# High and low weight parts interleaved element by element in one buffer, in a one-core decoder step

## What is computed

```
proj = rmsnorm(x) @ w_in          # 2048 -> 7168: short convolution and retention, 8 heads
out  = concat(y_conv, y_ret) @ w_out
x    = x + out
q    = rmsnorm(x) @ w_q           # product-key router: 8 heads, top 16 of 16384 experts each
hid  = gelu(h @ u_tab.T)          # here for all 16384 experts, gates are 0 for those not picked
x    = x + (gate * hid) @ v_tab   # then a last rmsnorm
```

## Time and profile before

| what | value |
|---|---|
| time, median of 3 runs | 2122.25 us (2121.98 to 2123.11) |
| span of the profiled execution | 2120.7 us |
| TensorE matmul busy | 2099.2 us, 99% |
| TensorE weight load busy | 2087.6 us, 98% |
| VectorE busy | 1441.5 us, 68% |
| ScalarE busy | 963.0 us, 45% |
| GpSimd busy | 68.4 us, 3% |

### The profile page before, as it was taken

The page is one execution under the profiler, slowest core; times in us unless marked ns, Lnnn a source line. Parts: engine busy times, 40 slices in busy tenths (PEclk is TensorE's granted clock), DMA queues, the critical chain, the costliest instruction groups (busy, mean ns, idle before and its releaser), DMA issues.

```text
span 2120.7 us, 46483 instructions
## 1 busy us (share of the span) xinstructions
PE 2099.2 (99%) x18585; PEld 2087.6 (98%) x18585; DVE 1441.5 (68%) x2700; ACT 963.0 (45%) x1343; POOL 68.4 (3%) x94
## 2 busy tenths in 40 slices
PE   8999999999999999999999999999999999999997
PEld 8999999999999999999999999999999999999997
DVE  8888876568888677755656656565645556666665
ACT  6666533444534344443434344443434344444444
POOL 1111000000000000000000000000000000000000
PEclk9999999999999999999999999999999999999999
DMA  8666555654455556675556565565656566656653
GB/s 296 222 217 216 189 180 182 199 176 152 159 188 179 179 189 213 207 245 184 195 198 212 187 213 196 195 204 194 212 188 205 174 216 203 215 202 201 205 180 123
DMA packets 115175, 418.39 MB, mean 197 GB/s; under 512 B 13600, under 2 KB 14112, under 8 KB 114752
## 3 DMA queue, kind: packets, MB, share of 16 engines
q1 hardware_dynamic: 100800, 365.29, 52.2%
q0 software_dynamic: 9888, 34.47, 5.0%
q10 hardware_dynamic: 4320, 16.22, 2.0%
HBM read 391.55 MB, written 24.29 MB: 196 GB/s over the span
## 4 chain that ended last, share of the span: by engine, by line
PE 98%; DVE 1%; ACT 0%; DMA 0%; issue 0%; DVEq 0%; SPq 0%; ACTq 0%
PE bank L929 32%; PE bank L930 31%; PE bank L931 31%; PE bank L1102 2%; PE bank L1057 1%; DVE wlo L1181 0%; PE bank L1002 0%; DMA acc<-xT 0%; DVE acc L1871 0%; PE bank L1013 0%; PE bank L1009 0%; PE bank L977 0%; PE bank L987 0%; PE bank L961 0%; DVE outer L1273 0%
## 5 line engine op out<-in xcount | busy, mean ns | idle before, releaser
L1181 DVE TENSOR_TENSOR wlo<-raw,whi 128x1024 fp32r<-128x1024 f32 x688 | 830.5, 1223 | 500.4 <-ACT whi L634 496.5
L634 ACT CAST whi<-raw 128x1024 fp32r<-128x1024 f32 x688 | 710.2, 1048 | 630.8 <-PE bank L931 624.7
L929 PE MATMUL bank<-xhi,whi 128*128 128x264 f32 x3200 | 911.5, 285 | 0.0
L930 PE MATMUL bank<-xlo,whi 128*128 128x264 f32 x3200 | 906.7, 283 | 0.0
L931 PE MATMUL bank<-xhi,wlo 128*128 128x264 f32 x3200 | 906.5, 283 | 0.0
L930 PEld LDWEIGHTS bank<-xlo,whi 128*128 128x128 f32 x3200 | 603.1, 188 | 0.0
L929 PEld LDWEIGHTS bank<-xhi,whi 128*128 128x128 f32 x3200 | 602.6, 188 | 0.2 <-issue 0.2
L931 PEld LDWEIGHTS bank<-xhi,wlo 128*128 128x128 f32 x3200 | 600.1, 188 | 0.0
L929 PE MATMUL bank<-xghi,whi 128*128 128x264 f32 x1152 | 333.5, 289 | 9.5 <-DVE wlo L1181 9.5
L929 PE MATMUL bank<-wexp_hi,whi 128*128 128x264 f32 x1152 | 328.0, 285 | 0.0
L930 PE MATMUL bank<-xglo,whi 128*128 128x264 f32 x1152 | 327.4, 284 | 0.0
(11 more groups left out here) (216 smaller groups left out, 1125.0 us busy)
## 6 DMA issues: line engine op xcount, KB each, us to landing
raw<-halves SPq DMA_DIRECT2D x688, 512.0 KB, 3.4
hid<-gates ACTq DMA_DIRECT2D x30, 528.0 KB, 4.9
gates<-stage POOLq DMA_DIRECT2D x17, 768.0 KB, 7.1
s_old<-ret_state POOLq DMA_DIRECT2D x8, 512.0 KB, 7.4
vs_all<-values POOLq DMA_DIRECT2D x8, 512.0 KB, 5.6
ret_sample<-s_new POOLq DMA_DIRECT2D x8, 512.0 KB, 4.2
gates<-route_mem POOLq DMA_DIRECT2D x5, 768.0 KB, 7.4
acc<-xT SPq DMA_DIRECT2D x4, 528.0 KB, 6.3
```

The costliest lines, as they stand in the source:

```text
L634: nc.scalar.copy(whi[:, s], raw[:, s]).then_inc(hi_done, 1)
L929: nc.tensor.matmul(out, whi[:, s, c], mh[c], start=start and c == 0, stop=False)
L930: nc.tensor.matmul(out, whi[:, s, c], ml[c], start=False, stop=False)
L1181: v.tensor_tensor(wlo[:, s], raw[:, s], whi[:, s].bitcast(F32), ALU.subtract).then_inc(lo_done, 1)
```

## The change

The two buffers `whi` and `wlo` become one, `both`, with a last dimension of 2: a high part at the even places, its low part right behind it. `whi` and `wlo` are now views of it with a step of two elements (8 bytes). No other line changes: ScalarE writes with a step of two, VectorE reads the high parts and writes the low parts with a step of two, and TensorE loads its 128 x 128 blocks with a step of two along the free dimension. The size in memory is the same (twice 16 KB a partition before, once 32 KB now), and the buffer takes the place of the two.

```
--- before.py
+++ after.py
@@ -216,8 +216,8 @@
         raw = sb("raw", [P, RING, HALF, P])
-        whi = sb("whi", [P, RING, HALF, P], F32R)
-        wlo = sb("wlo", [P, RING, HALF, P], F32R)
+        both = sb("both", [P, RING, HALF, P, 2], F32R)
+        whi, wlo = both[:, :, :, :, 0], both[:, :, :, :, 1]
```

## The result

The changed kernel takes 2154.5 us (median, 2154.17 to 2155.0), against 2122.25 us before: 32 us slower, a ratio of 1.0151 with a 95% interval of 1.0139 to 1.0163. The profiled execution spans 2152.9 us, 32.2 us more than before, so the profile shows the whole difference.

A forecast was written before the change was run, and what follows sets the result against it. The prediction took TensorE's 16,512 load-and-matmul pairs, 0.1205 us each, as the bound. Its terms for loads, VectorE and ScalarE summed 0 + 0 + 0: 2122 us, no change (chance 0.62), range 2105 to 2300 us.

The forecast's parts named there:

- the 7% to spare: TensorE's weight load, at 0.111 to 0.113 us, was put some 0.008 us below the 0.1205 us load-and-matmul pair, or with no slack.
- I take 0 us: TensorE's 16,512 weight loads with a step of two were claimed to cost nothing; ends: nothing or up to 0.120 us each.
- The sign named for a wrong prediction: Any of the three accesses taking more than a tenth longer with short cover: none for the load, about 0.5 us for L1181.
- Rival 1: TensorE's weight loads run at half or nearly half rate and set the pace, deciding from 0.1205 us a load; chance 0.17.
- The slow form: TensorE's stepped load takes 0.202 us (factor 1.79) or 0.233 us (0.94 ns an element more): 3470 or 3980 us in all.
- The mild form: TensorE's stepped load takes only 0.125 us, adding 16,512 x 0.0045 = 74 us.
- VectorE's low part, 0 us: L1181's strided read and write, 688 times, were claimed likely to cost nothing; otherwise 0.96 us an instruction, 1.92 if both cost.
- Rival 2: Loads free, but VectorE's strided low part becomes the bound: 2200 to 2280 us expected, to 2777 if both cost; chance 0.15.
- The rule of adjacent pairs: VectorE's port keeps full rate only for runs of two or more adjacent 4-byte words; it put L1181 at 2.0 us or more.
- ScalarE's high part, 0 us: L634's strided write, 688 times, was claimed likely to cost nothing; at 0.96 us more each, 661 us of ScalarE work.
- The cover named for it: ScalarE's 630.8 us idle at L634, plus the ring of slots giving TensorE three halves, 8.7 us, of work ahead.
- Rival 3: Adjacent high and low parts suit TensorE's loads, so the pair falls towards the load's pace: down to 1998 us; chance 0.06.

## Why the prediction was wrong

**What bounds the kernel: right.** The pair of load and matmul sets the end, at 0.1205 us; the load's own pace was read as 0.111 to 0.113 us from a one-column matmul, the run with 216 columns measured 0.1124, and the bare plain load 0.1115. "A load that is slower by more than that lengthens every pair", said of the 7% to spare, was the right worry with the wrong threshold: a load slower by 6% did it already.

**TensorE's loads, "I take 0 us": here it failed.** The load has one element in 0.87 ns to fetch, and I took the free 4-byte step of VectorE's L1750 as the nearest row for an 8-byte step. The stepped load costs 6 ns by itself, 2 ns of it in the pair, 32 us in all. Two things were wrong in it. The price was taken as one of two values, free or 0.94 ns an element, while it grows with the lines touched, and at two elements a line it lies just above what the load needs anyway. And the time to spare was treated as a full cover: "it decides from 0.1205 us a load on". The stepped load takes 0.1175 us bare and 0.1189 us at 216 columns, under that threshold, and a third of its 6 ns came through. The sign named for a wrong prediction, an access that takes more than a tenth longer, would have missed it too: 6% in the load's pace were enough.

**Rival 1: the right place, the wrong size.** The slow form (3470 to 3980 us) did not come for a step of two; it came, 9 us above its upper end, for a step of four (3989 us). That its 0.94 ns an element, taken from a VectorE row, nearly hit TensorE's load there (0.234 us after 0.233) is not explained by any run. The mild form was worked out as 74 us for a load of 0.125 us; the change cost 32 us. The rivals' chance of 0.17 for a cost in the loads was too small against 0.62 for none, in a kernel whose load had 7% to spare at most.

**VectorE's low part, 0 us: right.** 1224 ns after 1223, for a strided read and a strided write of floats together. Rival 2 is refuted. The rule of adjacent pairs that stood beside it, from the Trainium skill (Vector Engine (DVE) Microarchitecture Reference, section 5.2), does not hold for a step of 8 bytes here.

**ScalarE's high part, 0 us: wrong in the row, right in the sum.** Its strided write costs 95 ns. The cover named for it, its idle time for TensorE and the ring, holds: the run with stepped writes alone takes 2122.66 us.

**Rival 3, faster: it did not come.** High and low parts side by side gave the loads nothing; the pair got longer.

**The range** of 2105 to 2300 us holds 2154.5 us; the likeliest case, no change, did not come.

## What to carry to other kernels

When two pipelined parts of one engine lie within some per cent of one another, the shorter one's time to spare is not free: a cost that would fit into it still came through by a third, and in one arrangement in full. Such a cost can be measured by taking work from the longer part until the shorter one is bare; here 48 columns fewer turned 2 ns into 6. And before a stationary operand gets a step, count the 16-byte lines it touches: at the 1.85 ns a line of these fp32r loads at 2.4 GHz, two floats a line is already a little more than a plain load takes, and one float a line nearly doubles the pair.

## What the runs showed of the hardware that was not expected

A stream of loads with matmuls of 32 columns keeps TensorE busy for 99% of the span, yet its granted clock was 0.5, the 1.2 GHz level, nearly throughout. In the run with plain loads and 32 columns, from 1200 to 1300 us, then in the run with the step (count, then the clock):

```profile
1200.00:1300.00 100.00, 100.00 (x467) 0.50 0.33 102
```

```profile
1200.00:1300.00 100.00, 100.00 (x467) 0.50 0.32 105
```

With 216 columns the stretch from 1800 to 1900 us shows 1.00. So 216 columns made the kernel 130 us faster and 32 columns made it 1567 us slower (3688.87 against 2122.25 us).

At the low clock the step of two was free. Either run takes 100 / 467 = 0.214 us a pair, well above the 118 ns that 64 lines took at the high clock; if a line's price had doubled with the slower clock, to 237 ns, the step would have shown. The two totals still differ by 21 us, which is not the step's price: in the plain run the clock came back twelve times and in the other six, and the plain run has 832 distances under 150 ns between neighbouring matmuls of the tiles, the other 643. At some 0.1 us less for each, the 189 more make about 20 us.

The record of the clock has a gap that one has to know. Before its first entry it reads 1.00: until past 300 us in the run with the step, and in the first slice of the page above. But the loads at 249.67 and 251.81 us are ten steps of 0.214 us apart, and in the plain run those at 79.68 and 81.82 us are, too. So the first 9 of that PEclk row is no full clock, and the distance of the starts is the safer witness.

```profile
249.67 0.33 PEld L936 LDWEIGHTS bank<-xghi,both 128*128 128x128 f32 x1
...
251.81 0.33 PEld L937 LDWEIGHTS bank<-xglo,both 128*128 128x128 f32 x1
```

ScalarE and VectorE differ over the same step: writing every second float costs ScalarE 9% (1143 after 1048 ns), and VectorE, which also reads with the step, nothing.
